# Splitting weights further ahead, own PSUM banks for the gates, and a mixer whose head pairs are issued in turns

## The reference

```python
h = rmsnorm(x, norm_mix)
proj = h @ w_in
(z, xbc, dt_raw, lru_y, lru_x, q, k, v, ret_g, gate_pre) = jnp.split(proj, offsets, axis=-1)
# RG-LRU
xb = causal_dwconv(lru_x, lru_conv_w, lru_conv_b)
r = jax.nn.sigmoid(block_diagonal(xb, w_a) + b_a)
i = jax.nn.sigmoid(block_diagonal(xb, w_i) + b_i)
log_a = -8.0 * r * softplus(-lam)
h_lru = associative_scan(exp(log_a), sqrt(-expm1(2 * log_a)) * (i * xb))
y_lru = h_lru * gelu(lru_y)
# SSD mixer: 16 heads of 64, chunks of 128 positions
xs, bm, cm = split(silu(causal_dwconv(xbc, ...)))
dt = softplus(dt_raw + dt_bias)
y_ssd = chunked_state_space_mixer(xs * dt, dt * a, bm, cm) + xs * d_skip
```

## Time and profile before

| what | value |
|---|---|
| median of three runs | 3189.16 us |
| the three runs | 3189.16, 3189.72, 3175.99 us |
| profiled execution, its own time | 3174.15 us |
| its span, first to last instruction | 3172.3 us |
| PE busy | 3086.7 us, 97% |
| DVE busy | 1813.3 us, 57% |
| ACT busy | 938.4 us, 30% |
| POOL busy | 285.0 us, 9% |
| mean granted clock of PE | 0.988 |

### The profile page before, as it was taken

How to read it: one execution, slowest core, us unless ns; L and a number is a source line. 1 busy time by engine, 2 the same in 40 slices (tenths; PEclk the granted TensorE clock), 3 DMA queues, 4 the chain that set the end, 5 groups by cost and what they waited for, 6 DMA issues and landing times.

```text
span 3172.3 us, 37089 instructions
## 1 busy us (share of the span) xinstructions
PE 3086.7 (97%) x13759; PEld 2494.0 (79%) x13759; DVE 1813.3 (57%) x2421; ACT 938.4 (30%) x1285; POOL 285.0 (9%) x135
## 2 busy tenths in 40 slices
PE   7999999999999999999999999999999999999999
PEld 6778778768788887888877888887888887588887
DVE  8786445267766555555576755445554446565442
ACT  3553633233222222222222222222222244322222
POOL 0034231220000000000042000002000031000000
PEclk9999999999999999999999999999999998999999
DMA  3222123213222232223331222232223321022232
GB/s 131 91 86 90 50 73 115 90 55 113 93 99 93 99 100 85 94 95 104 113 100 54 99 97 96 99 107 93 93 96 103 115 68 40 14 93 99 99 106 86
DMA packets 79373, 287.67 MB, mean 91 GB/s; under 512 B 9056, under 2 KB 9312, under 8 KB 78880
## 3 DMA queue, kind: packets, MB, share of 16 engines
q1 hardware_dynamic: 77328, 278.03, 26.3%
q0 software_dynamic: 1936, 8.13, 0.8%
HBM read 284.02 MB, written 2.10 MB: 90 GB/s over the span
## 4 chain that ended last, share of the span: by engine, by line
PE 77%; issue 14%; DVE 4%; POOL 3%; ACT 1%; DMA 0%; POOLq 0%; DVEq 0%; ACTq 0%
PE ps L605 24%; PE ps L606 24%; PE ps L607 24%; POOL w_lo L559 3%; PE ps L698 1%; PE ps L714 1%; PE ps L1137 1%; PE ps L998 1%; PE ps L1143 0%; PE ps L764 0%; PE ps L1136 0%; DVE rstd L1659 0%; ACT w_hi L1181 0%; DVE w_lo L1595 0%; PE ps L1004 0%
## 5 line engine op out<-in xcount | busy, mean ns | idle before, releaser
L605 PE MATMUL ps<-h_hi,w_hi 128*128 128x512 f32 (+1 forms) x2443 | 962.9, 394 | 16.7 <-ACT tmp L1185 7.8
L607 PE MATMUL ps<-h_hi,w_lo 128*128 128x512 f32 (+1 forms) x2443 | 951.9, 390 | 0.0
L606 PE MATMUL ps<-h_lo,w_hi 128*128 128x512 f32 (+1 forms) x2443 | 951.8, 390 | 0.0
L1181 ACT ACTIVATE w_hi<-raw 128x1024 fp32r<-128x1024 f32 x525 | 555.1, 1058 | 1307.9 <-PE ps L607 1303.9
L1595 DVE TENSOR_TENSOR w_lo<-raw,w_hi 128x1024 fp32r<-128x1024 f32 x415 | 507.4, 1223 | 446.2 <-ACT w_hi L1181 445.6
L605 PEld LDWEIGHTS ps<-h_hi,w_hi 128*128 128x128 f32 x2443 | 461.7, 189 | 124.1 <-issue 18.2
L607 PEld LDWEIGHTS ps<-h_hi,w_lo 128*128 128x128 f32 x2443 | 461.4, 189 | 96.0
L606 PEld LDWEIGHTS ps<-h_lo,w_hi 128*128 128x128 f32 x2443 | 461.7, 189 | 95.4 <-issue 2.6
L605 PE MATMUL ps<-mid_hi,w_hi 128*128 128x512 f32 x1208 | 471.4, 390 | 2.2 <-DVE mid_lo L1670 2.1
L606 PE MATMUL ps<-mid_lo,w_hi 128*128 128x512 f32 x1208 | 470.7, 390 | 0.0
L607 PE MATMUL ps<-mid_hi,w_lo 128*128 128x512 f32 x1208 | 470.4, 389 | 0.0
(11 more groups left out here) (391 smaller groups left out, 2534.7 us busy)
## 6 DMA issues: line engine op xcount, KB each, us to landing
raw<-in_wstream SPq DMA_DIRECT2D x525, 512.0 KB, 3.3
x<-in_x SPq DMA_DIRECT2D x8, 256.0 KB, 5.5
x_in<-in_x POOLq DMA_DIRECT2D x8, 256.0 KB, 3.0
mem_x<-in_mem POOLq DMA_DIRECT2D x2, 1024.0 KB, 5.0
out<-x POOLq DMA_DIRECT2D x8, 256.0 KB, 3.5
tmp<-in_ret_decay POOLq DMA_DIRECT2D x1, 1024.0 KB, 5.0
rope_r<-in_rope_r POOLq DMA_DIRECT2D x1, 512.0 KB, 3.8
mats<-in_mats SPq DMA_DIRECT2D x1, 320.0 KB, 6.4
```

The source lines that it names most:

```text
L605: nc.tensor.matmul(dst, hi_w, hi_x, start=first, stop=False)
L606: nc.tensor.matmul(dst, hi_w, lo_x, start=False, stop=False)
L607: return nc.tensor.matmul(dst, lo_w, hi_x, start=False, stop=last)
L1181: nc.scalar.activation(w_hi[:, n % HL], raw[:, r], ACT.Copy).then_inc(hi_ready, 1)
```

## The change

It edits four places; everything behind ssd_y is as before.

In lru_x and gate1, ACT's split of panel 3 stands ahead of the root, and DVE's split of panel 3 ahead of the reciprocal; DVE's loop splits panel c + 4 at tile c in place of panel c + 3 (c + 2 later on). ACT makes `xb_hi`, in gate1, and reads each gate1 tile one turn later; DVE keeps only `xb_lo` (`lru_low`), which waits for ACT's copy (`xb_cast`).

In lru, the four gate tiles go to the banks 4 to 7 and the y tiles to two of the banks 0 to 3 (`lru_bank`).

In dt, ACT splits br1's second panel ahead of the softplus' exponential.

In ssd_y, PE issues the spreads up to four heads ahead, `y_diag` takes both heads of a pair and goes from one to the other at each chunk, `y_carried` uses banks 6 and 7 in turn from pair 4 on, and `pair_out` and `pair_in` come a pair later.

The banks of lru's tiles:

```diff
+        def lru_bank(b, m):
+            return ps[:, AUX + m] if m < 4 else ps[:, (2 * b + m) % BANKS]
```

PE in lru:

```diff
                 for m in range(4):
-                    bank_free(t + m)
+                    if b:
+                        pe.wait_ge(drained, t + m - 5)
                     for k in range(2):
-                        mm = three(bank(t + m), *blocks(n, 2 * m + k), xb_hi[:, 2 * b + k], xb_lo[:, 2 * b + k],
+                        mm = three(lru_bank(b, m), *blocks(n, 2 * m + k), xb_hi[:, 2 * b + k], xb_lo[:, 2 * b + k],
                                    k == 0, k == 1)
                 mm.then_inc(panel_done, 1)
                 for j in range(2):
-                    tile_part(n + 1 + j, t + 4 + j, h_hi, h_lo, 0, 1, KB)
+                    pe.wait_ge(lo_of(n + 1 + j), split_count(n + 1 + j))
+                    pe.wait_ge(drained, t + j - 7 if b >= 2 else st.t)
+                    for k in range(KB):
+                        mm = three(lru_bank(b, 4 + j), *blocks(n + 1 + j, k), h_hi[:, k], h_lo[:, k], k == 0, k == KB - 1)
+                    mm.then_inc(panel_done, 1)
```

PE in ssd_y:

```diff
-            def y_diag(hd):
-                t, rows, feats = y_tile(hd // 2), slice(SSD_P * (hd % 2), SSD_P * (hd % 2) + SSD_P), slice(SSD_P * hd, SSD_P * hd + SSD_P)
-                if hd % 2 == 0:
-                    bank_free(t)
-                pe.wait_ge(m_ready, hd + 1)
+            def y_diag(p):
+                t = y_tile(p)
+                bank_free(t)
+                pe.wait_ge(m_ready, 2 * p + 2)
                 for c in range(CH):
-                    mm = nc.tensor.matmul(bank(t)[rows, P * c:P * c + P], xs_tok[:, c, feats],
-                                          decay[:, hd % 4, P * c:P * c + P], start=True, stop=True)
-                mm.then_inc(y_done, 1)
+                    for e in range(2):
+                        rows, f = slice(SSD_P * e, SSD_P * e + SSD_P), SSD_P * (2 * p + e)
+                        mm = nc.tensor.matmul(bank(t)[rows, P * c:P * c + P], xs_tok[:, c, f:f + SSD_P],
+                                              decay[:, (2 * p + e) % 4, P * c:P * c + P], start=True, stop=True)
+                        if c == CH - 1:
+                            mm.then_inc(y_done, 1)
...
+            spread(2)
+            spread(3)
             for p in range(DT):
-                if p + 1 < DT:
-                    spread(2 * p + 2)
-                y_diag(2 * p)
+                if p + 2 < DT:
+                    spread(2 * p + 4)
                 if p == 0:
                     chunk_state(0, 2, 6)
                 if p + 2 < DT:
                     gate_tile(p + 2)
-                if p + 1 < DT:
-                    spread(2 * p + 3)
-                y_diag(2 * p + 1)
+                    spread(2 * p + 5)
+                y_diag(p)
                 if 1 <= p <= 3:
                     chunk_state(1, p - 1, 7)
                 if p:
```

ACT in lru_x and gate1:

```diff
             split(2)
             act.wait_ge(consts_ready, 1)
+            split(3)
             root()
...
             st = ST["gate1"]
             for j in range(DT):
                 split(st.n + j + 1)
-                if j == 0:
+                act.wait_ge(taps_done, j + 1)
+                nc.scalar.activation(xb_hi[:, j], xb[:, j], ACT.Copy).then_inc(xb_cast, 1)
+                if j == 1:
                     act.wait_ge(drained, st.t)
-                drain(st.n + j, st.t + j, sg[:, j], func=ACT.Sigmoid)
+                if j:
+                    drain(st.n + j - 1, st.t + j - 1, sg[:, j - 1], func=ACT.Sigmoid)
+            drain(st.n + DT - 1, st.t + DT - 1, sg[:, DT - 1], func=ACT.Sigmoid)
```

ACT in dt:

```diff
+            split(n + 2)
             act.wait_ge(sp_in, 2)
             nc.scalar.activation(decay[0:16, 1], decay[0:16, 1], ACT.Exp).then_inc(sp_exp, 1)
```

ACT in ssd_y:

```diff
-                elif hd % 2 == 0 and hd:
-                    pair_out(hd // 2 - 1)
-            pair_out(SSD_HEADS // 2 - 1)
+                elif hd % 2 == 0 and hd >= 4:
+                    pair_out(hd // 2 - 2)
+            pair_out(DT - 2)
+            pair_out(DT - 1)
```

DVE in lru_x and gate1, with the function that takes the place of `lru_halves`:

```diff
+            def lru_low(c):
+                dve.wait_ge(xb_cast, c + 1)
+                v.tensor_tensor(xb_lo[:, c], xb[:, c], xb_hi[:, c].bitcast(F32), ALU.subtract).then_inc(conv_done, 1)
...
             ins.then_inc(squares_summed, 1)
+            split(3)
             reciprocal_root()
...
-                elif c > 4:
-                    lru_halves(c - 5)
-                if c != 3:
-                    split(st.n + c + (3 if c < 3 else 2))
+                split(st.n + c + 4)
                 if c < 4:
                     mix_tile(2 * c + 1)
                 else:
                     dve.wait_ge(drained, st.t + c - 3)
                     lru_taps(c - 4)
+                    if c > 4:
+                        lru_low(c - 5)
...
-            for j in range(DT):
-                if j < 5:
-                    lru_halves(3 + j)
-                if j < DT - 1:
-                    split(st.n + j + 2)
+            for j in range(5):
                 if j < 4:
                     dve.wait_ge(drained, ST["lru_x"].t + 5 + j)
                     lru_taps(4 + j)
+                if j < 3:
+                    split(st.n + j + 4)
+                lru_low(3 + j)
+            for j in range(3, 5):
+                split(st.n + j + 4)
```

DVE in ssd_y:

```diff
                 masked(hd)
-                if hd % 2 == 0 and hd >= 4:
-                    if hd <= 8:
-                        carry(1, hd // 2 - 2, 7)
-                    pair_in(hd // 2 - 2)
+                if hd % 2 == 0 and 6 <= hd <= 10:
+                    carry(1, hd // 2 - 3, 7)
+                if hd % 2 == 0 and hd >= 6:
+                    pair_in(hd // 2 - 3)
+            pair_in(DT - 3)
             pair_in(DT - 2)
             pair_in(DT - 1)
```

More of the change, by code:

```diff
@@ L380, in build @@
         u_ready = sem("u_ready")
+        taps_done = sem("taps_done")
+        xb_cast = sem("xb_cast")
         squares_summed = sem("squares_summed")
@@ L885, in chunk_state, with carried_bank @@
                     .then_inc(state_done, 1)
+            def carried_bank(p):
+                return 6 + p % 2 if p >= 4 else 6
             def y_carried(p):
@@ L1181, in split, with drain @@
                 nc.scalar.activation(w_hi[:, n % HL], raw[:, r], ACT.Copy).then_inc(hi_ready, 1)
[L1183 removed]
+            def drain(n, t, dst, i=None, step=0, tstep=0, func=ACT.Copy, rows=slice(0, P), cols=S, bias=0.0, scale=1.0, src=None):
                 act.wait_ge(panel_done, at(n + 1, i, step))
[L1185 removed]
+                src = bank(t) if src is None else src
+                nc.scalar.activation(dst, src[rows, 0:cols], func, bias=bias, scale=scale).then_inc(drained, 1)
             def stage_slot(s, i=None, step=0):
@@ L1278, in _ @@
             nc.scalar.activation(small[:, 24:32], small[:, 24:32], ACT.Exp).then_inc(sp_exp, 1)
-            for n in range(2, ST["lru_x"].panels):
-                split(n + 1)
+            for n in range(4, ST["lru_x"].panels + 1):
+                split(n)
             st = ST["gate1"]
@@ L1338, in _ @@
             drain(n, t, decay[0:16, 0], func=ACT.Identity, rows=slice(0, 16), bias=vcol("ssd_dt_bias", 0)[0:16])
+            split(n + 2)
             act.wait_ge(sp_in, 2)
             nc.scalar.activation(decay[0:16, 1], decay[0:16, 1], ACT.Exp).then_inc(sp_exp, 1)
-            gemm("br1", to_stage("br1"))
+            st = ST["br1"]
+            for j in range(DT):
+                if j:
+                    split(st.n + j + 1)
+                drain(st.n + j, st.t + j, stage_slot(st.s + j))
             st = ST["ssd_y"]
@@ L1830, in lru_taps @@
                     later = dst[:, back:]
-                    done(v.scalar_tensor_tensor(out=later, in0=src[:, 0:S - back], scalar=w[3 - back], in1=later,
-                                                op0=ALU.mult, op1=ALU.add))
-            def lru_halves(c):
-                halves(xb_hi[:, c], xb_lo[:, c], xb[:, c], conv_done)
+                    ins = v.scalar_tensor_tensor(out=later, in0=src[:, 0:S - back], scalar=w[3 - back], in1=later,
+                                                 op0=ALU.mult, op1=ALU.add)
+                    if back < 3:
+                        done(ins)
+                ins.then_inc(taps_done, 1)
+            def lru_low(c):
+                dve.wait_ge(xb_cast, c + 1)
+                v.tensor_tensor(xb_lo[:, c], xb[:, c], xb_hi[:, c].bitcast(F32), ALU.subtract).then_inc(conv_done, 1)
             def mix_tile(k):
@@ L1985, in pair_in @@
                 dve.wait_ge(grown_done, 2 * p + 2)
-                done(v.tensor_tensor(late, late, ps[:, 6, P:S], ALU.mult))
+                done(v.tensor_tensor(late, late, ps[:, 6 + p % 2 if p >= 4 else 6, P:S], ALU.mult))
                 drained_tile(st.t + (2 + 2 * p if p < DT - 2 else DT + p))
```

14 lines of the change are left out of this document (8 added, 6 removed).

## The result

The changed kernel takes 3169.7 us (median of nine runs, 3161.9 to 3172.12) against 3186.36 us of the kernel before in nine runs (3175.99 to 3189.72): the ratio is 0.995, with a 95% interval of 0.9936 to 0.9965. The forecast was 3168 us, in a range from 3153 to 3184. The profiled execution took 3161.9 us, 12.25 us less than the one before, against the 14.1 us of the sum.

The account below looks back on a forecast made before the run. PE has work for nearly all of the edited 420 us, with 24 us of waits. Terms 5.5 + 4.8 + 1.9 + 1.9 = 14.1 us take 3174.15 to 3160; with scatter to 3175, the middle, 3168 us, was predicted, range 3153 to 3184.

Parts of the forecast that it names:

- First stage and gate1: +5.5 us: lru_x and gate1: the end moves by 9.8 us, less new waits of 0.6 and 3.7 us.
- the wait at panel 15: gate1's last panel: PE waits 3.7 us for DVE's split, queued behind the last `xb_lo` and ACT's copy.
- lru: +4.8 us: lru: four waits, 7.8 us, go; 1.0 us of late `w_lo` comes, and xbc takes back 2.0 us.
- The reason given: xbc: DVE has little slack, so an earlier PE waits for DVE's reading of the tiles, 2.0 us.
- dt: +1.9 us: dt: PE's wait of 1.9 us for br1's second panel goes, as its split precedes an exponential.
- which hide it: dt: the exponential, 1.1 us later, feeds only ssd_y, so br1's eight panels of 5.44 us hide the delay.
- ssd_y: +1.9 us: ssd_y: products 8.2 won, spreads' waits 9.5 lost, old tail waits 6.5 won, last pair's wait 3.3 lost.
- The clock: 0: Slower-clock stretches: four go with their waits, about four come with new ones; net 0, ends +6.8 and -3.4 us.
- The first, serial halves: ssd_y: the products' halves stay serial, 7.2 of 8.2 us are lost, gain 7, 3175 us; chance 0.10.
- The third, more meetings of DVE and POOL: xbc: DVE meets POOL's splits more often, 2.1 us each; twelve more give 3193 us; chance 0.06.
- The second, new waits smaller than chained: gate1's 4.3 us don't come, or only two slower stretches return; gain 17 to 21, 3162 us; chance 0.35.
- the bound that was set: Whole kernel: 0.5% (16 us) is about what a measurement can tell from no change; the bound lies at 3173 us.

Follow-up runs that it names:

- the first stage alone: The kernel before with the edits of lru_x and gate1 only; ratio 0.9991 (0.9976 to 1.0007) against the kernel before.

## Why the prediction was right

The stages won 3.8, 6.2, 2.2 and -0.1 us where the sum had 5.5, 4.8, 1.9 and 1.9. The misses have both signs, so that 12.1 us at z for a sum of 14.1 owes something to luck. So does the time: of the 21 us from 3189 to 3168 us, 14.1 were the sum and 7 the place in the scatter where the medians would fall; of the measured 16.7 us 10 to 12 are the change.

**First stage and gate1: +5.5 us, without the clock.** It came out as worked: 9.8 us, less the wait at panel 15 (3.58 for 3.7) and one of 0.38 for 0.6 us; the slower matmuls behind the former (1.7 us) are what parts 5.5 from the 3.8 of the table. That the queue's order alone made this wait is shown by moving one split.

**lru: +4.8 us.** The four waits went, and they come back with the shared banks. Of the small waits, for which I took 1.0 in lru, none came there; 0.36 and 0.22 us came at xbc's first panels. In xbc a wait of 0.79 us for a bank (as it stands again with the shared banks) gave way to one of 2.34 us for POOL's split, 1.6 more where I took 2.0. By the waits that makes 5.7 us, and one slower stretch fewer brought the rest of the 6.2. The reason given was wrong in part. DVE's lag was there, but four banks can hold it; PE waited because ACT's split stood behind a read that waited for DVE. With the split ahead of it the wait is gone, and no wait for a bank comes in its place.

**dt: +1.9 us.** The step "which hide it" failed. Not ssd_y alone needs the chain: DVE's sums for br1 stand behind it, and so do transposes on PE. The old wait went, and its slower stretch; 1.21 us came in at the fourth panel. The stage won 2.2 us.

**ssd_y: +1.9 us, and -0.1 in the trace.** The terms were right in size: 8.6 us won on the products (17.4 to 8.8 us of busy time) for 8.2; 9.5 us of waits for the spreads (1.42, 2.55, 2.32, three of 0.60, 1.45) for 9.5; 3.01 us at the last pair for 3.3. With the 6.5 us of old waits the stage should have won 2.6 us by them. Most of what is missing is the clock: it fell at the mixer's start (2.0 us, by 0.50 over 4 us) and behind the 2.32 us wait (1.7 us), and one stretch of before went (1.7 us), which makes 2.0 us. For the last 0.7 us I have no row.

**The clock: 0.** Four slower stretches went besides the one counted in the first stage. After, it fell behind the waits at 99.5, 199, 321 and 335 us, so it cancelled as assumed.

**The rivals.** The first, serial halves, did not happen: issued in turns, the halves overlap, as the earlier trace rows said. Its price of 7.2 us is in doubt, too: products issued one head after the other, which take 1.58 us, cost 0.6 us in this kernel, for the waits on ACT take up what the products leave. Products that do not overlap at all, which the rival meant, were not run. So in the changed kernel the turns themselves bring almost nothing. With the spreads as before, where no such wait stands between, the whole stage is 92.67 - 82.07 = 10.6 us shorter than before; how much of this the turns bring was not run apart from the shorter tail. The third, more meetings of DVE and POOL, is refuted: the twelve tiles' taps keep DVE busy for 46.1 + 8.6 = 54.7 us in xbc, where they took 48.5 + 6.5 = 55.0 before (lines 1720 and 1718 of the changed kernel, 1688 and 1686 before, 180 to 260 us), and 11 of these 48 operations are longer than 2.6 us in both:

```profile
L1720 DVE SCALAR_TENSOR_TENSOR xbc<-cpad,vec,xbc 128x512 f32 x36 | 46.1, 1282 | 5.4 <-DVE xbc L1718 1.5 <-DVE xbc L1720 1.5
L1718 DVE TENSOR_SCALAR xbc<-cpad,vec 128x512 f32 x12 | 8.6, 718 | 3.1 <-ACT cpad L1204 3.1
...
L1688 DVE SCALAR_TENSOR_TENSOR xbc<-cpad,vec,xbc 128x512 f32 x36 | 48.5, 1347 | 5.4 <-DVE xbc L1686 1.5 <-DVE xbc L1688 1.5
L1686 DVE TENSOR_SCALAR xbc<-cpad,vec 128x512 f32 x12 | 6.5, 544 | 1.5 <-ACT cpad L1185 1.5
```

The second, new waits smaller than chained, did not happen; those that were chained came within 0.3 us of it, and four slower stretches came back, not two. By time, the kernel is 0.5% faster, at the bound that was set.

## What to carry to other kernels

Issuing an operation earlier gains only if what it waits for is earlier too. The spreads four heads ahead stood in PE's queue on banks that ACT had not freed, and so held up a gate panel that had no need of them; put where their banks are free, they leave the stage 10.7 us shorter. A wait in an in-order queue is best read as: what stands behind it that needn't? A split behind a half of another tile (gate1) and one behind a read (xbc) were the answer here, and exchanging two lines took each wait away; in br1 the same exchange only moved the wait, as the earlier split ran beside the DVE chain that PE needed next and made it longer.

When a term takes a wait away, follow the producer of what comes next as far as its next consumer: the softplus' chain was no longer than before, but PE reached it 3.6 us earlier and waited there.

## What the runs showed of the hardware

Two matmul groups that write different halves of 64 columns overlap even if issued one after the other: 16 records take 1.58 us where apart they take 2 x 1.02 us, and 1.09 us when issued in turns. I had expected 2.0. The rule of the Trainium skill in "TensorE: Matmul & The Clock Gate", Part 3, "What overlaps and what doesn't", is that weight loads overlap running matmuls only where the row group differs. By it the order should make no difference for halves in columns, and that does not agree with the 1.58 and 1.09 us.

The same wait does not always bring the slower clock. Behind the 3.6 us at gate1's last panel it fell in all seven profiles that have this wait; behind the 2.3 us in xbc in three of six; behind the last pair's 3.0 to 3.3 us in seven of eight, the changed kernel's profile being the one without. The scatter of one kernel's runs goes with this clock. Of the 53 runs of the kernel before that were made beside the experiments, those with a mean granted clock of 0.988 took 3173.5 to 3174.9 us, those with 0.982 3188.0 to 3188.7 us. From z's wait to the end, the same code took 2754.3 us in the changed kernel's profile and 2764.4 us in that of the first stage alone, with mean clocks over the span of 0.988 and 0.985. No run sets the clock, so that it is the cause is argued and not shown. A change of a few microseconds is therefore told by the place where it acts, not by one time.
